# Two-layer hybrid transformer, one core: the first rows arrive turned as well, their squares are summed on GpSimd

## The reference, cut to what matters

```python
h = rms_norm(x, norm1_g[l])        # x * rsqrt(mean(x*x) + EPS) * g, over the 1024 columns
z = h @ w_in[l]                    # 1024 x 8704
```

```python
x = x + sigmoid(rms_norm(x, g) @ ple_gate[l]) * (p[l] @ ple_proj[l])
```

## Time and profile before

| | |
|---|---|
| median of three runs | 2411.31 us |
| the profiled execution | 2411.47 us, span 2410.2 us |
| TensorE busy | 2385.8 us (99%), 12156 matmuls |
| VectorE busy | 1761.7 us (73%) |
| ScalarE busy | 1493.6 us (62%) |
| GpSimd busy | 86.2 us (4%) |
| DMA | 612.42 MB, mean 254 GB/s |
| TensorE's share of the chain that ended last | 94% |

### The profile page before, as it was taken

The page is one execution under the profiler, slowest core; times in us unless marked ns, Lnnn a source line. Parts: engine busy times, 40 slices in busy tenths (PEclk is TensorE's granted clock), DMA queues, the critical chain, the costliest instruction groups (busy, mean ns, idle before and its releaser), DMA issues.

```text
span 2410.2 us, 30624 instructions
## 1 busy us (share of the span) xinstructions
PE 2385.8 (99%) x12156; PEld 2016.4 (84%) x12156; DVE 1761.7 (73%) x2181; ACT 1493.6 (62%) x1955; POOL 86.2 (4%) x106
## 2 busy tenths in 40 slices
PE   9999999999999999999999999999999999999998
PEld 7888899888889998888888888888888888888887
DVE  6755655577466556565456579999999999999997
ACT  6455544544555445654446667777777777777775
POOL 0000100000000000100000200000000000000001
PEclk9999999999999999999999999999999999999999
DMA  8444565544446555355454379999999999999992
GB/s 308 155 161 140 177 244 190 181 169 158 157 150 209 179 173 173 120 173 184 156 192 161 120 281 389 395 393 378 384 380 382 378 385 377 387 379 381 377 388 98
DMA packets 268416, 612.42 MB, mean 254 GB/s; under 512 B 12472, under 2 KB 17958, under 8 KB 268268
## 3 DMA queue, kind: packets, MB, share of 16 engines
q1 hardware_dynamic: 263788, 594.71, 69.0%
q0 software_dynamic: 4320, 15.49, 1.6%
q10 hardware_dynamic: 160, 0.20, 0.0%
HBM read 599.59 MB, written 11.01 MB: 253 GB/s over the span
## 4 chain that ended last, share of the span: by engine, by line
PE 94%; DVE 3%; ACT 1%; POOL 1%; issue 0%; DMA 0%; DVEq 0%; ACTq 0%; POOLq 0%
PE PS L780 24%; PE PS L782 24%; PE PS L781 24%; PE PS L839 3%; PE PS L835 3%; PE PS L837 2%; PE PS L768 1%; PE PS L761 1%; PE PS L763 1%; DVE WL L2260 1%; PE PS L1383 1%; PE PS L882 1%; PE PS L891 1%; PE PS L996 1%; PE PS L965 1%; PE PS L1218 1%
## 5 line engine op out<-in xcount | busy, mean ns | idle before, releaser
L2260 DVE TENSOR_TENSOR WL<-raw,WH 128x1024 fp32r<-128x1024 f32 (+2 forms) x796 | 930.6, 1210 | 293.7 <-ACT WH L1677 288.3
L1677 ACT CAST WH<-raw 128x1024 fp32r<-128x1024 f32 (+2 forms) x796 | 792.5, 1042 | 326.4 <-PE PS L782 281.6
L780 PE MATMUL PS<-WH,XTH 128*128 128x512 f32 (+2 forms) x1952 | 771.9, 395 | 0.1
L782 PE MATMUL PS<-WH,XTL 128*128 128x512 f32 (+2 forms) x1952 | 755.4, 387 | 0.0
L781 PE MATMUL PS<-WL,XTH 128*128 128x512 f32 (+2 forms) x1952 | 753.7, 386 | 0.0
L782 PEld LDWEIGHTS PS<-WH,XTL 128*128 128x128 f32 x1952 | 366.5, 188 | 76.1
L780 PEld LDWEIGHTS PS<-WH,XTH 128*128 128x128 f32 x1952 | 366.9, 188 | 73.4 <-issue 2.7
L781 PEld LDWEIGHTS PS<-WL,XTH 128*128 128x128 f32 x1952 | 367.4, 188 | 69.2
L2260 DVE TENSOR_TENSOR WL<-AR,WH 128x1024 fp32r<-128x1024 f32 x334 | 391.6, 1221 | 27.1 <-ACT WH L1677 26.1
L1677 ACT CAST WH<-AR 128x1024 fp32r<-128x1024 f32 x334 | 334.3, 1052 | 66.1 <-PE PS L782 65.9
L780 PE MATMUL PS<-WH,HTH 128*128 128x512 f32 x706 | 275.0, 390 | 1.1 <-DVE HTL L2952 1.1
(11 more groups left out here) (354 smaller groups left out, 1965.0 us busy)
## 6 DMA issues: line engine op xcount, KB each, us to landing
raw<-in_w_in SPq DMA_DIRECT2D x91, 1024.0 KB, 5.1
raw<-in_moe_w_gate SPq DMA_DIRECT2D x57, 1024.0 KB, 7.6
raw<-in_moe_w_up SPq DMA_DIRECT2D x57, 1024.0 KB, 7.8
AR<-in_moe_w_down SPq DMA_DIRECT2D x57, 1024.0 KB, 7.9
AR<-in_moe_w_gate SPq DMA_DIRECT2D x55, 1024.0 KB, 7.6
AR<-in_moe_w_up SPq DMA_DIRECT2D x55, 1024.0 KB, 7.9
raw<-in_moe_w_down SPq DMA_DIRECT2D x55, 1024.0 KB, 8.2
raw<-in_w_up SPq DMA_DIRECT2D x32, 1024.0 KB, 5.5
```

The lines of the kernel that those rows point to most:

```text
L780: pe.matmul(o, lh, rh, start=start, stop=False, skip_group_check=True)
L782: return pe.matmul(o, ll, rh, start=False, stop=stop, skip_group_check=True)
L1677: act.copy(WH[:, i % WR, c], slots[s][:, c]).then_inc(*wh.inc(i, h))
L2260: dve.tensor_tensor(WL[:, i % WR, c], slots[s][:, c], WH[:, i % WR, c].bitcast(F32), ALU.subtract).then_inc(*wl.inc(i, h))
```

## The change

x is also laid out turned in device memory (`x_turned`, 1024 x 256), p only turned, and the first norm's gain as a column of 128 x 8. SP loads the first half of the turned x (`XR`) first of all, the identity behind weight piece 1, and natural x (1 MB, one transfer) ahead of weight piece 10; VectorE waits for that before the first residual add. The transposes of x at the start, of the gain and of the identity go; TensorE begins with 13 matmuls of a tile of ones (`WAKE`), which GpSimd sets. ScalarE and VectorE make the high and low parts from `XR` in SBUF, each in two chunks at a time. ScalarE's squares of natural x go: GpSimd squares the turned x in two halves and adds 2048 columns down to 256; TensorE, before the second group, waits for that (`xsq`) and sums over the partitions with two matmuls against a column of ones; VectorE, before its part of the second group, waits for these (`xsum`) and scales them; GpSimd makes the root. The second group uses banks 2 and 3. The parts of p are made from `PP` in SBUF, without transposes.

```diff
 def sync():
-            sp.dma_start(CF[:, 0:128], cf[:, 0:128]).then_inc(ld_i, 16)
-            sp.dma_start(X[:, :, 0:512], xv[:, :, 0:512]).then_inc(ld_x, 16)
+            xv = dr["x_turned"].rearrange("(c p) m -> p c m", p=P)
+            sp.dma_start(XR[:, 0:4, :], xv[:, 0:4, :]).then_inc(ld_x, 16)
...
-            sp.dma_start(X[:, :, 512:1024], xv[:, :, 512:1024]).then_inc(ld_y, 16)
+            sp.dma_start(XR[:, 4:8, :], xv[:, 4:8, :]).then_inc(ld_y, 16)
...
+                    if j == 2:
+                        sp.dma_start(CF[:, 0:128], cf[:, 0:128]).then_inc(ld_i, 16)
+                    if j == first[("in1", 0, 5)]:
+                        sp.dma_start(X[:, :, :], dr["x"][0].rearrange("(t p) d -> p t d", p=P)).then_inc(ld_n, 16)
 def gpsimd():
+            pool.memset(WAKE, 1.0).then_inc(*woke.inc(0))
...
-            root(rs, ss, ("n1", 0), ssq.at("n1", 0))
+            xr = XR.rearrange("p c m -> p (c m)")
+            for h, loaded in enumerate((ld_x, ld_y)):
+                hs_ = slice(1024 * h, 1024 * h + 1024)
+                pool.wait_ge(loaded, 16)
+                pool.tensor_tensor(XQ[:, hs_], xr[:, hs_], xr[:, hs_], ALU.mult).then_inc(*own.inc())
+            for n in (1024, 512, 256):
+                pool.wait_ge(*own.now())
+                m = pool.tensor_tensor(XQ[:, 0:n], XQ[:, 0:n], XQ[:, n:2 * n], ALU.add)
+                m.then_inc(*(xsq.inc(0) if n == 256 else own.inc()))
+            root(rs, ss, ("n1", 0), ssq0.at(0))
 def tensor():
-            pe.wait_ge(ld_i, 16)
-            pe.wait_ge(ld_g0, 16)
-            pe.transpose(PS[:, 7, 0:8], G0, ident[0:8, 0:8]).then_inc(*gt.inc(0))
-            free[7] = gcol.at(0)
-            awake(14)
-            half(("n1", 0), X, 0, ((ld_x, 16), None))
-            awake(8)
+            pe.wait_ge(*woke.at(0))
+            for _ in range(13):
+                pe.matmul(PS[:, 2, 0:P], WAKE, WAKE, start=True, stop=True)
...
+                    b0 = 2 if (l, g) == (0, 1) else 4
+                    if (l, g) == (0, 1):
+                        pe.wait_ge(*xsq.at(0))
+                        bank(0)
+                        for t in range(T):
+                            m = pe.matmul(PS[:, 0, t:t + 1], XQ[:, t * P:t * P + P], WAKE[:, 0:1], start=True, stop=True)
+                        m.then_inc(*xsum.inc(0))
+                        free[0] = ssq0.at(0)
 def scalar():
-            act.wait_ge(*gcol.at(0))
-            for r in range(2):
-                half(("n1", 0), 0, gain4(("n1", 0), 0), only=(r,))
-                split(0, r)
-            half(("n1", 0), 1, gain4(("n1", 0), 1), b0=0)
+            act.wait_ge(ld_g0, 16)
+            for h, r in ((0, 0), (0, 1), (1, 0), (1, 1)):
+                if r == 0:
+                    act.wait_ge(ld_y if h else ld_x, 16)
+                for c in range(4 * h + 2 * r, 4 * h + 2 * r + 2):
+                    m = act.activation(XTH[:, c, :], XR[:, c, :], ACT.Copy, scale=gc(("n1", 0), c))
+                m.then_inc(*xh.inc("n1", 0, h, r))
+                if h == 0:
+                    split(0, r)
             split(1, 0)
             split(1, 1)
-            norm(("n1", 0), (ld_x, 16), (ld_y, 16))
...
+            def ple_high(l):
+                act.wait_ge(ld_p[l], 16)
+                act.copy(PTH[:, :, :], PP).then_inc(*xh.inc("pt", l, 0, 0))
 def vector():
+            for h, r in ((0, 0), (0, 1), (1, 0), (1, 1)):
+                dve.wait_ge(*xh.at("n1", 0, h, r))
+                for c in range(4 * h + 2 * r, 4 * h + 2 * r + 2):
+                    m = dve.scalar_tensor_tensor(out=XTL[:, c, :], in0=XR[:, c, :], scalar=gc(("n1", 0), c),
+                                                 in1=XTH[:, c, :].bitcast(F32), op0=ALU.mult, op1=ALU.subtract)
+                m.then_inc(*xl.inc("n1", 0, h, r))
+                if h == 0:
+                    split(0, r)
...
+                    if (l, g) == (0, 1):
+                        dve.wait_ge(*xsum.at(0))
+                        dve.tensor_scalar(ss, PS[:, 0, 0:2], 1.0 / D, None, ALU.mult).then_inc(*ssq0.inc(0))
...
+            def ple_low(l):
+                dve.wait_ge(*xh.at("pt", l, 0, 0))
+                dve.tensor_tensor(PTL[:, :, :], PP, PTH[:, :, :].bitcast(F32), ALU.subtract).then_inc(*xl.inc("pt", l, 0, 0))
```

More of the change, by code:

```diff
@@ L322, in program @@
         OA = ar(15360, 1024).rearrange("p (t n) -> p t n", t=2)
-        G0 = AR[0:8, 16256:16384]
+        XR = ar(2560, 2048).rearrange("p (c m) -> p c m", c=8)
+        WAKE = ar(4608, 128)
+        XQ = ar(4736, 2048)
         HM = ar(15360, 1024).rearrange("p (t n) -> p t n", t=2)
@@ L439, in program @@
         ld_i, ld_g0, ld_x, ld_y, ld_c, ld_g, ld_m, ld_rd = (sem("ld_" + x) for x in ("i", "g0", "x", "y", "c", "g", "m", "rd"))
-        ld_h = sem("ld_h")
+        ld_h, ld_n = sem("ld_h"), sem("ld_n")
+        woke, xsq, xsum, ssq0 = sig("woke", 1), sig("xsq", 1), sig("xsum", 1), sig("ssq0", 1)
         ld_f1, ld_f2, ld_p0, ld_p1, ld_o0, ld_o1, s_out = (sem(x) for x in ("ld_f1", "ld_f2", "ld_p0", "ld_p1", "ld_o0", "ld_o1", "s_out"))
@@ L449, in program @@
                  for r in range(1 if k[0] == "pt" else 2)]
-        tx, xh, xl = sig("tx", turns), sig("xh", turns), sig("xl", turns)
-        NORMS = [("n1", 0), ("n2", 0), ("n1", 1), ("n2", 1), ("nf", 0), ("pn", 0), ("nm", 1), ("nf", 1), ("pn", 1), ("last", 0),
+        tx = sig("tx", [k for k in turns if k[0] != "pt" and k[:2] != ("n1", 0)])
+        xh, xl = sig("xh", turns), sig("xl", turns)
+        NORMS = [("n2", 0), ("n1", 1), ("n2", 1), ("nf", 0), ("pn", 0), ("nm", 1), ("nf", 1), ("pn", 1), ("last", 0),
                  ("last", 1), ("last", 2)]
@@ L789, in blocks, with group @@
                 return [w[:, k, c] for k in range(w.shape[1])]
-            def group(key, n, nk=2, k0=0, banks=(4, 5), early=None):
+            def group(key, n, nk=2, k0=0, banks=(4, 5), early=False):
                 for i, kp, t in lane.up(key, nk):
                     a, b = piece(i)
-                    begins = early is not None and (kp, t) == (0, 0)
+                    begins = early and (kp, t) == (0, 0)
                     if t == 0:
@@ L884, in half @@
                     free[b0 + r] = xl.at(*key, h, r)
-                    if key[0] != "pt":
-                        turned[2 * h + r] = xh.at(*key, h, r), xl.at(*key, h, r)
+                    turned[2 * h + r] = xh.at(*key, h, r), xl.at(*key, h, r)
             def heads(src, b, wd=P):
@@ L1063, in awake @@
                     pe.transpose(PS[:, 2, 0:P], ident, ident)
-            pe.wait_ge(ld_i, 16)
-            pe.wait_ge(ld_g0, 16)
-            pe.transpose(PS[:, 7, 0:8], G0, ident[0:8, 0:8]).then_inc(*gt.inc(0))
-            free[7] = gcol.at(0)
-            awake(14)
-            half(("n1", 0), X, 0, ((ld_x, 16), None))
-            awake(8)
+            pe.wait_ge(*woke.at(0))
+            for _ in range(13):
+                pe.matmul(PS[:, 2, 0:P], WAKE, WAKE, start=True, stop=True)
+            for c in range(4):
+                turned[c] = xh.at("n1", 0, c // 2, c % 2), xl.at("n1", 0, c // 2, c % 2)
             for l in range(2):
@@ L1076, in tensor @@
                         lane.until(("hgrn", l))
-                    rest = (lambda: half(("n1", 0), X, 1, ((ld_y, 16), None), b0=0)) if (l, g) == (0, 0) else None
-                    for kp, t in group(("in1", l, g), 512, early=rest):
+                    b0 = 2 if (l, g) == (0, 1) else 4
[6 more added lines that the diff above has]
+                        free[0] = ssq0.at(0)
+                    for kp, t in group(("in1", l, g), 512, banks=(b0, b0 + 1), early=(l, g) == (0, 0)):
                         if (l, g, kp, t) == (1, 0, 0, 0):
@@ L1253, in retention @@
                 yield
[L1255 to L1258, removed]
             def ple_product():
@@ L1599, in tensor @@
                 lane.drain()
-                if l:
-                    half(("pt", 1), PP, 0, ((ld_p[1], 16), None), 0, 2, b0=0)
                 for n in range(2):
@@ L1619, in tensor @@
                 if l == 0:
-                    lane.side.append(ple_turn())
                     mlp("m2", 0, FF2, ("nf", 0))
@@ L1711, in head_task @@
                         act.wait_ge(*rsd.at("n1", l))
-                    act.mul(ZT[:, t, :], PS[:, 4 + t, :], rs[:, t:t + 1]).then_inc(*ev1.inc(l, g, t))
+                    act.mul(ZT[:, t, :], PS[:, (2 if (l, g) == (0, 1) else 4) + t, :], rs[:, t:t + 1]).then_inc(*ev1.inc(l, g, t))
                 yield
@@ L1834, in mlp @@
                             pass
-            act.dma_start(G0, dr["norm1_g"][0].rearrange("(c p) -> c p", p=P)).then_inc(ld_g0, 16)
-            act.wait_ge(ld_i, 16)
-            act.activation(sm[:, 252:253], ident[:, 0:1], ACT.Copy, scale=ident[:, 0:1])
-            act.wait_ge(*gcol.at(0))
-            for r in range(2):
-                half(("n1", 0), 0, gain4(("n1", 0), 0), only=(r,))
-                split(0, r)
-            half(("n1", 0), 1, gain4(("n1", 0), 1), b0=0)
```

(23 more changed lines are left out.)

20 lines of the change are left out of this document (9 added, 11 removed).

## The result

The changed kernel takes 2415.27 us (2414.47 to 2416.37) where the kernel before takes 2411.31 (2410.55 to 2412.10) beside it: ratio 1.0017, 95% interval 1.0011 to 1.0022. It is 4.0 us slower, or 0.17%: clear of no change by the interval, but under the 0.2% (2416.1 us) from which the prediction calls a kernel slower. Its profiled execution took 2415.24 us with a span of 2413.9; before, 2411.47 and 2410.2.

The account below looks back on a forecast made before the run. TensorE was taken to bound the kernel, loose only before the second matmul group: +6.3 us at that start, +1.9 for the clock, -0.9 for p, +7.3 on the median 2411.31, gave 2418.6 us, range 2410.5 to 2421.0.

Parts of the forecast that it names:

- Part 4, exclusion: Before the second group: GpSimd's 9.4 us and VectorE's 12.3 us add instead of overlapping; start at 27.7, +6.3 us.
- rival B: Before the second group: engines exclude, but GpSimd gets in between VectorE's instructions; start +4.0, 2414.4 to 2416.3 us; chance 0.2.
- rival A: Before the second group: GpSimd and VectorE overlap, sums done at 16.8, start +0.5; 2410.9 us, or 2409.4; chance 0.18.
- sign for A: In the profile's start: squares ending before 17 us would show that GpSimd and VectorE overlap.
- sign for B: In the profile's start: VectorE's and GpSimd's instructions alternating would show that GpSimd gets in between.
- Part 4, the scaled subtraction: Low parts of x at the start: VectorE's scaled subtraction, reading two SBUF tiles, also stands behind GpSimd's first square.
- Part 3: GpSimd's chain before the second group: two squares and an add at 2.37 us, adds of 1.25 and 0.69; 9.4 us.
- Part 5: TensorE's first two pieces: clock still low, first 12 to 14 matmuls 0.43 us each, pieces ending at 16.1 and 21.6.
- The 19.0 "at best": Earliest second-group start, from the first cast's end at 8.05 and 48 matmuls taking 10.9 us.
- Part 6: After TensorE's stand from 21.6 to 27.4: the clock falls to 1.2 GHz, costing +1.9 us, bounds 0 and 3.5.
- Parts 1, 2 and 7: Arrivals (turned half at 5.5), VectorE's 12.3 us queue before its new wait, p's transposes gone (-0.9), natural x costing nothing.

Follow-up runs that it names:

- e1: The changed kernel with GpSimd's two squares and three adds replaced by five memsets of 2048 columns, which read nothing: 2409.26 us, ratio 0.9991.
- e4: The changed kernel with GpSimd's second square, and so its adds, waiting for the low parts of weight piece 1: 2416.57 us, ratio 1.0022.
- e6: The changed kernel with the squares on ScalarE and the adds on VectorE, GpSimd making only the root: 2409.08 us, ratio 0.9991.
- e3: The changed kernel with 20 matmuls of the tile of ones ahead of TensorE's wait for piece 1's low parts: 2413.38 us, ratio 1.0010.
- e2: The changed kernel with GpSimd's second square made twice, same result: 2417.61 us, ratio 1.0026.
- e5: The kernel before with only p laid out turned and its parts made from SBUF, without transposes: 2410.32 us, ratio 0.9997.

## Why the prediction was right, and where it was not

It gave 2418.6 us in a range of 2410.5 to 2421.0; measured were 2415.27. The direction held, and so did the main part of the mechanism: the two engines exclude each other, and the stand costs the clock as well. The place of the stand did not. That the time lies inside the range says little, as the range reaches from below the kernel before to nearly 10 us above it; and by the prediction's own line at 2416.1 the outcome is "same", which had 0.33, and not "slower", which had 0.64.

Of the 3.3 us of error 3.0 lie in the start without the clock (+6.3 forecast, +3.3 measured) and 0.3 in the clock. By the prediction's own sum, as an estimate, the earlier arrival of x makes 0.4 of the 3.0, the two shorter squares 1.0, which leaves 1.6 for the order in which the engines take turns.

**Part 4, exclusion: right. Its order and its size: wrong, and this is the step that failed.** I let GpSimd in only when VectorE's row of ready instructions broke, so that the second square began at 15.8, the adds behind the low parts of piece 3, and the start came at 27.7. In fact GpSimd got in after one VectorE instruction each time, as rival B said. The adds were done at 17.30, which is as early as rival A had them, but VectorE had given the time away, ahead of the second weight piece. TensorE's wait for xsq cost nothing; the loss was at a wait that was there before. I had looked at the queue behind the new waits and not asked enough who waits for the VectorE instructions that GpSimd holds up. B's price for the start was +4.0, with the clock +4.0 to +5.9; measured +4.86, so the time lies inside B's 2414.4 to 2416.3, in part by luck, as the stand is at another place than B's too. e1 shows the exclusion (5.9 us at the start). e4 puts the second square where I had it, behind the low parts of piece 1: TensorE then does stand at the new wait, but 4.64 us and not 5.8, because the adds still get in between VectorE's instructions. My sign for A, squares that end before 17 us, didn't separate the cases: taken by its words it came true, at 12.50, and the sums ended at 17.30, yet A is wrong. The sign for B, engines that alternate, came true.

**Part 4, the scaled subtraction: right.** Its first pair, beside the first square, took 1.61 us, and in e1, beside no reader, a pair took 0.88. The rule of the Trainium skill (SBUF — State Buffer, Who interferes with whom) held here for both of VectorE's forms with two SBUF inputs: the scaled subtraction, and the plain one (1.21 us alone, up to 3.41 in e4).

**Part 3, GpSimd's durations: right for the adds, too high for the squares.** Adds: 2.44, 1.34 and 0.79 against 2.37, 1.25 and 0.69, with 0.2 us of standing behind VectorE in each of the first two. The square of 1024 columns, whose two inputs are the same tile, took 1.89 against 2.37.

**Part 5, the clock at the start: wrong, and it went the other way.** The 13 warm-up matmuls stand in the trace as 26, lasting from 0.99 to 6.4, where I had them done at 3.8 and the clock low at the first piece. It was up: nearly all matmuls of the first piece take 0.39 to 0.40 us where they take 0.63 at half clock, and the piece ends at 14.3, not at 16.1. This is why e1 and e6, in which nothing excludes, come out at A's lower end, 2409.4 (measured 2409.26 and 2409.08). The prediction gives that figure without its terms; they are the second weight piece at 12.5, its cast 1.04, its low part 1.14, 24 matmuls 5.5 and the sums 0.3, a start at 20.5 (20.44 in e1). The 19.0 "at best" leaves that piece out.

**Part 6, the clock after the stand: right in size, at another place.** +1.9 predicted; 1.7 by the stretches, 1.4 to 1.6 by e3. It was lost in the second piece and not behind the start.

**Parts 1, 2 and 7: right, but for one reading.** Weight low parts took 1.21 us each, six in a row 6.89 (1.14 each predicted). The turned half issued at 0.73 was there at about 5.1, when the square began (5.5 predicted). The earlier trace rows has 4.7 us for rows of 2 KB; rows of 1 KB took 4.3, and in e2, where the square began at 5.5, some 4.7: no longer in either case. p: -0.94 measured, -0.9 predicted. Natural x, with the rest of what e1 keeps, left the start 1.0 us early; no cost of it shows. The reading was wrong there: natural x is issued at 32.9, when the DMA engines are fully busy (share 1.04 to 1.05 from 30 to 40 us, before and after) and not half, and it lands 9.8 us later; TensorE doesn't stand between 30 and 120 us.

In one line, at the start of the second group: -1.0 from the earlier input and the warm-up (e1), +4.3 from VectorE's delay (18.77 against 14.50, where e1 begins the second piece), +1.6 from the clock: 4.9, less 0.9 for p: +4.0.

## What to carry to other kernels

Before work goes to an idle GpSimd, look at what VectorE does in that stretch: if its instructions read two SBUF tiles, the two engines' times add up, and the idle engine is no free one. Then ask who waits for the VectorE instruction that is held up, not only who waits for GpSimd. ScalarE did the same squares beside VectorE at no cost, and VectorE itself had room for the adds. A stand of some microseconds on TensorE has a second price behind it, and the clock can fall after the work has resumed, in a stretch in which nothing else looks wrong.

## What the runs showed of the hardware

- **Who gets in isn't fixed.** Large GpSimd instructions at the start took turns one for one with VectorE's in the changed kernel, e2, e3 and e4. The small operation on two columns that opens the root at 2386.99 in before has the same neighbours in all runs, a row of four weight low parts, and begins 1.3 us behind the first of them in each. It took 3.42 or 3.43 us in before, e1, e4 and e6, and 1.15 in the changed kernel, e2, e3 and e5. Order in time, GpSimd, in e6:

```profile
2384.72 3.42 POOL L645 TENSOR_SCALAR sm<-sm 128x2 f32<-128x2 f32 x1 [64.72 <-ACT XN L1703]
```

and in the changed kernel:

```profile
2391.05 1.15 POOL L644 TENSOR_SCALAR sm<-sm 128x2 f32<-128x2 f32 x1 [64.75 <-ACT XN L1711]
```

  I know of no difference in their code there that would decide it; what does is open. From the start of this operation to the end of the span it is 23.1 to 23.2 us in the first four kernels and 22.8 to 22.9 in the others, so some 0.3 us of a difference between two profiled executions can come from here.
- **A memset on GpSimd doesn't hold VectorE**, nor does ScalarE's square: four low parts in 1.66 and 1.67 us beside them.
- **The clock fell after work had resumed**: in the changed kernel 0.65 us behind the first matmul after a stand of 4.5 us, in e4 0.7 us behind the one after 4.6; in e2, with 6.1, it fell 1.8 us ahead of it. Before the end of before it had fallen between 2406.0 and 2406.5, behind a last matmul at 2403.0. So a stand that ends is no proof that the clock held.
- **Matmuls on the tile of ones stand twice in the trace**: 13 of 128 columns in the code are 26, 20 are 40 (4.62 us, 0.116 each at the full clock), and the two of one column that sum the squares are four. Transposes (8 are 8) and the products with parts in fp32r (24 a piece) stand once.
